# Dilated attention with its first group in natural token order, a selection-product exchange of maxima and sums, and the last head inside the output units

## The reference, cut to what matters

```
for g, (window, dilation) in enumerate(((128, 1), (512, 4), (2048, 16))):
    q = apply_partial_rope(proj[:, :, g, 0], positions) * scale
    k = apply_partial_rope(proj[:, :, g, 1], positions)
    v = proj[:, :, g, 2]
    o, lse = dilated_window_attention(q, k, v, window, dilation)
    outs.append(o); lses.append(lse)
wts = softmax(stack(lses), axis=0)
o = einsum('gbsh,gbshd->bshd', wts, stack(outs))
return o.reshape(B, S, ATTN_WIDTH) @ w_out
```

## Time and profile before

| what | us |
| --- | --- |
| median of 3 runs (2657.55 to 2659.01) | 2658.34 |
| the profiled execution | 2656.87 |
| its span | 2655.1 |
| TensorE busy | 2507.8 (94%) |
| GpSimd busy | 1661.0 (63%) |
| VectorE busy | 1556.2 (59%) |
| ScalarE busy | 481.2 (18%) |

### The profile page before, as it was taken

How to read it: one execution, slowest core, us unless ns; L and a number is a source line. 1 busy time by engine, 2 the same in 40 slices (tenths; PEclk the granted TensorE clock), 3 DMA queues, 4 the chain that set the end, 5 groups by cost and what they waited for, 6 DMA issues and landing times.

```text
span 2655.1 us, 33809 instructions
## 1 busy us (share of the span) xinstructions
PE 2507.8 (94%) x12073; PEld 2028.7 (76%) x12073; DVE 1556.2 (59%) x1655; ACT 481.2 (18%) x832; POOL 1661.0 (63%) x700
## 2 busy tenths in 40 slices
PE   6998999997999997899999989999999998999997
PEld 4776776775888875788888868888887676887886
DVE  5867334685463467767666555434588466644446
ACT  4533221103000003111111121000141442100000
POOL 4435445674777774566666647877777423777784
PEclk7999999997999998999999999999999988999998
DMA  6212343421332322222222213323322101332331
GB/s 242 72 63 70 133 153 115 147 73 56 96 102 87 106 84 85 65 72 79 72 76 74 78 49 95 110 80 95 108 84 88 48 24 48 95 107 83 95 105 54
DMA packets 56332, 236.90 MB, mean 89 GB/s; under 512 B 6528, under 2 KB 7176, under 8 KB 52400
## 3 DMA queue, kind: packets, MB, share of 16 engines
q1 hardware_dynamic: 54720, 230.51, 27.2%
q10 hardware_dynamic: 1520, 5.16, 0.5%
HBM read 233.55 MB, written 2.10 MB: 89 GB/s over the span
## 4 chain that ended last, share of the span: by engine, by line
PE 83%; DVE 8%; ACT 2%; issue 2%; DVEq 2%; ACTq 1%; POOL 1%; DMA 1%; POOLq 0%
PE gg L514 19%; PE gg L515 19%; PE gg L516 19%; PE babcd L551 2%; PE babcd L553 2%; PE babcd L552 2%; PE gg L887 2%; PE be L1022 2%; PE gg L888 1%; PE gg L889 1%; PE babcd L514 1%; PE babcd L515 1%; PE babcd L516 1%; PE babcd L1006 1%; PE babcd L1091 1%
## 5 line engine op out<-in xcount | busy, mean ns | idle before, releaser
L444 POOL TENSOR_TENSOR w_hi<-raw,zero 128x1024 fp32r<-128x1024 f32 (+2 forms) x280 | 585.6, 2092 | 618.3 <-PE gg L516 460.6
L446 POOL TENSOR_TENSOR w_lo<-raw,w_hi 128x1024 fp32r<-128x1024 f32 (+2 forms) x280 | 756.8, 2703 | 39.9
L514 PE MATMUL gg<-h_hi,w_hi 128*128 128x512 f32 x1576 | 627.0, 398 | 9.7 <-ACT ff_s L1437 5.2
L515 PE MATMUL gg<-h_lo,w_hi 128*128 128x512 f32 x1576 | 620.7, 394 | 0.0
L516 PE MATMUL gg<-h_hi,w_lo 128*128 128x512 f32 x1576 | 619.6, 393 | 0.0
L514 PEld LDWEIGHTS gg<-h_hi,w_hi 128*128 128x128 f32 x1576 | 300.3, 191 | 78.5 <-issue 13.1
L516 PEld LDWEIGHTS gg<-h_hi,w_lo 128*128 128x128 f32 x1576 | 300.2, 190 | 63.8
L515 PEld LDWEIGHTS gg<-h_lo,w_hi 128*128 128x128 f32 x1576 | 300.4, 191 | 60.7
L1951 DVE TENSOR_TENSOR ta<-ff_s,gg 128x512 f32<-128x512 f32 x64 | 44.1, 689 | 331.2 <-PE gg L516 323.7
L435 POOL TENSOR_TENSOR w_hi<-raw,zero 128x1536 fp32r<-128x1536 f32 (+2 forms) x48 | 107.2, 2233 | 188.3 <-PE babcd L516 142.3
L514 PE MATMUL gg<-u_hi,w_hi 128*128 128x512 f32 x528 | 209.7, 397 | 4.2 <-issue 4.2
(11 more groups left out here) (530 smaller groups left out, 3998.8 us busy)
## 6 DMA issues: line engine op xcount, KB each, us to landing
raw<-in_w_ff_in_a SPq DMA_DIRECT2D x66, 512.0 KB, 3.6
raw<-in_w_ff_in_b SPq DMA_DIRECT2D x66, 512.0 KB, 3.6
raw<-in_w_att_qk SPq DMA_DIRECT2D x48, 512.0 KB, 3.6
raw<-in_w_ff_out_a SPq DMA_DIRECT2D x24, 704.0 KB, 4.1
raw<-in_w_ff_out_b SPq DMA_DIRECT2D x24, 704.0 KB, 4.1
late_raw<-in_w_ada SPq DMA_DIRECT2D x16, 1024.0 KB, 5.0
raw<-in_w_ml SPq DMA_DIRECT2D x25, 512.0 KB, 3.6
raw<-in_w_merge_a SPq DMA_DIRECT2D x16, 768.0 KB, 5.4
```

The source lines that it names most:

```text
L444: pool.tensor_tensor(hi, a, zero[:].to_broadcast([P, size * P]), ALU.add)
L446: pool.tensor_tensor(lo, a, hi, ALU.subtract).then_inc(S["units_split"], 1)
L514: pe.matmul(dst, w_hi[slot][:, blk], xs[0][:, k, :], start=k == 0, stop=False)
L515: pe.matmul(dst, w_hi[slot][:, blk], xs[1][:, k, :], start=False, stop=False)
```

## The change

The query and key of group 0 are kept in natural token order: projection_out writes them through by_token and by_residue (strided), with rope tables copied into that order. In natural order a block of 128 queries needs two blocks of keys (the first one), so group 0 has 7 blocks a head and groups 1 and 2 have 8: 15 in place of 24. The maxima and sums of the four natural blocks and of the four residues are held by different partitions for the same token. att_swap exchanges them by products with 0/1 matrices (sel_in, sel_out) after swap_in spreads them, and swap_out picks them. ScalarE takes the exp of both shifts (shifts), VectorE merges them (factors), then norm scales the eight parts. The values of group 0 are brought into natural order by four DMAs a head (v_n, from copy_values), and the output of its blocks is written into the residue order by a strided PSUM view. The attention of head h - 1 has its scores after projection unit 0, the exchange after unit 1, the transposes after unit 3 and the values after unit 4 of head h (all one unit later for head 1). The last head's attention runs within the first two output units (last_head). VectorE builds the selection matrices in feed_forward(0), in rope_phase at k == 4 and k == 6. The function tile_mm can be called without its wait.

The diff, cut (removed lines of the old functions are left out; they stand above):

```diff
+        def nat_scores(b):
+            return (ba, bb)[b // 2][:, b % 2 * 256 + (P if b == 0 else 0):b % 2 * 256 + 256]
+        def nat_part(b):
+            return slice(P if b == 0 else 0, 2 * P)
+        def res_scores(r):
+            return (bc, bd)[r // 2][:, r % 2 * 256:r % 2 * 256 + 256]
...
-                wait(pe, "att_scored", h * 4)
...
+            def att_scores(a, p):
+                pe.wait_ge(S["att_roped"], a * 6 + 6)
+                pe.wait_ge(S["att_v_out"], a + 1)
+                for b in range(TB):
+                    mm = pe.matmul(nat_scores(b), qk[p][:, 0, b * P:(b + 1) * P], qk[p][:, 1, max(b - 1, 0) * P:(b + 1) * P],
+                                   start=True, stop=True)
+                mm.then_inc(S["att_scores"], 1)
+                for r in range(4):
+                    tok = slice(r * P, (r + 1) * P)
+                    for n in range(2):
+                        mm = pe.matmul(res_scores(r)[:, n * P:(n + 1) * P], qk[p][:, 2 * n + 2, tok], qk[p][:, 2 * n + 3, tok],
+                                       start=True, stop=True)
+                mm.then_inc(S["att_scores"], 1)
+            def att_swap(a):
+                pe.wait_ge(S["att_expand"], a + 1)
+                y = swap_y[:, 0, :].rearrange("p (x r) -> p x r", x=8)
+                for b in range(TB):
+                    rows = slice(32 * b, 32 * b + 32)
+                    pe.matmul(bf[rows, 0:8], sel_in[:, rows], y[:, b:8:4, :], start=True, stop=True)
+                pe.matmul(bf[:, 8:40], sel_out[:], swap_y[:, 1, :], start=True, stop=True).then_inc(S["att_swapped"], 1)
+            def att_turn(a):
+                for bank, first, last, rows in ((ba, 0, 4, 3), (bb, 4, 7, 4)):
+                    pe.wait_ge(S["att_norm"], a * 8 + rows)
+                    for n in range(first, last):
+                        b, half = (n + 1) // 2, (n + 1) % 2
+                        mm = pe.transpose(bank[:, (n - first) * P:(n - first + 1) * P], p_nat[:, b, half * P:(half + 1) * P], ident[:])
+                    mm.then_inc(S["att_turned"], 1)
+                for q, bank in enumerate((bc, bd)):
+                    pe.wait_ge(S["att_norm"], a * 8 + (2 * q + 6))
+                    for n in range(4):
+                        r, half = 2 * q + n // 2, n % 2
+                        mm = pe.transpose(bank[:, n * P:(n + 1) * P], p_res[:, r, half * P:(half + 1) * P], ident[:])
+                    mm.then_inc(S["att_turned"], 1)
+            def att_values(a, p):
+                wait(pe, "att_o", a)
+                pe.wait_ge(S["att_pt"], a * 4 + 4)
+                pe.wait_ge(S["v_turned"], a * 64 + 64)
+                for r in range(4):
+                    for n in range(2):
+                        pe.matmul(be[:, r * P:(r + 1) * P], v_a[p][:, r, (n + 1) * P:(n + 2) * P], pt_res[:, (2 * r + n) * P:(2 * r + n + 1) * P],
+                                  start=r == 0 and n == 0, stop=False, skip_group_check=True)
+                for n in range(7):
+                    b, half = (n + 1) // 2, (n + 1) % 2
+                    mm = pe.matmul(by_residue(be[:])[:, 32 * b:32 * b + 32, :], v_n[p][:, b - 1 + half, :], pt_nat[:, n * P:(n + 1) * P],
+                                   start=False, stop=n == 6, skip_group_check=True)
                 mm.then_inc(S["att_values"], 1)
...
+            def att_step(a, p, s, at_step):
+                if s == at_step:
+                    att_scores(a, p)
+                if s == at_step + 1:
+                    att_swap(a)
+                if s == at_step + 3:
+                    att_turn(a)
+                if s == at_step + 4:
+                    att_values(a, p)
             def att_two(i):
                 for p in range(2):
                     h = i * 2 + p
                     for s in range(6):
                         if isinstance(h, int) and h == 0:
                             first_head(s)
...
+                            continue
+                        project(h, s)
+                        att_step(h - 1, 1 - p, s, int(isinstance(h, int)))
                     project_values(h)
             peeled(pe, 4, att_two)
...
-            residual("w_att_out", 8, (o_hi, o_lo), RES["att"], between=lambda k: pe.wait_ge(S["att_o"], k + 1))
+            def last_head():
+                u0 = FIRST["w_att_out"]
+                def unit(s, first, last):
+                    ready(u0 + s)
+                    for k in range(first, last):
+                        pe.wait_ge(S["att_o"], k + 1)
+                        tile_mm(g[(u0 + s) % 2], (u0 + s) % 2, k, (o_hi, o_lo))
+                pe.wait_ge(S["att_copied"], 48)
+                att_scores(7, 1)
+                unit(0, 0, 7)
+                att_swap(7)
+                unit(1, 0, 7)
+                att_turn(7)
+                att_values(7, 1)
+                unit(0, 7, 8)
+                unit(1, 7, 8)
+            residual("w_att_out", 8, (o_hi, o_lo), RES["att"], lead=last_head)
...
-            act.dma_start(att_mask[:], t["att_mask"]).then_inc(S["att_consts"], 16)
+            act.dma_start(mask_nat[:, 0:P], t["tri"]).then_inc(S["att_consts"], 16)
+            act.dma_start(mask_nat[:, P:2 * P], t["att_mask"][:, 0, 512:640]).then_inc(S["att_consts"], 16)
+            act.dma_start(mask_res[:], t["att_mask"][:, 0, 512:768]).then_inc(S["att_consts"], 16)
...
-                wait(act, "att_values", h * 4 - 4)
+                wait(act, "att_values", h - 1)
                 for b in range(TB):
                     act.activation(v_a[p][:, b, :], nat[b][:, 0:384], ACT.Copy, scale=colv[:, b:b + 1])
                 act.drain().then_inc(S["att_v_out"], 1)
...
+                wait(act, "att_v_out", h + 1)
+                for b in range(TB):
+                    act.dma_start(v_n[p][:, b, :], v_a[p][32 * b:32 * b + 32, :, 0:P]).then_inc(S["v_turned"], 16)
+            def expo(a):
+                for n in range(8):
+                    part = p_nat[:, n, nat_part(n)] if n < 4 else p_res[:, n - 4, :]
+                    m = n + n // 4 * 4
+                    wait(act, "att_scored", a * 8 + (n + 1))
+                    act.activation(part, part, ACT.Exp, scale=-1.0, bias=a_st[:, m:m + 1],
+                                   accum_out=a_st[:, m + 4:m + 5]).then_inc(S["att_exp"], 1)
+            def shifts(a):
+                wait(act, "att_shift", a + 1)
+                act.activation(a_st[:, 40:56], a_st[:, 40:56], ACT.Exp).then_inc(S["att_fexp"], 1)
+            def turned(a):
+                wait(act, "att_values", a)
+                for n, bank in enumerate((ba, bb[:, 0:3 * P], bc, bd)):
+                    to = (pt_nat[:, 0:4 * P], pt_nat[:, 4 * P:7 * P], pt_res[:, 0:4 * P], pt_res[:, 4 * P:8 * P])[n]
+                    wait(act, "att_turned", a * 4 + (n + 1))
+                    act.activation(to, bank, ACT.Copy).then_inc(S["att_pt"], 1)
+            def att_head(a):
+                expo(a)
+                shifts(a)
+                turned(a)
             def att_two(i):
                 for p in range(2):
                     h = i * 2 + p
...
+                    if not (isinstance(h, int) and h == 0):
+                        att_head(h - 1)
                     copy_values(h, p)
             peeled(act, 4, att_two)
...
+            att_head(7)
...
+            wait(v, "att_consts", 64)
+            v.tensor_copy(by_token(nat_c), by_residue(rope_c[:]))
+            v.tensor_copy(by_token(nat_s), by_residue(rope_s[:]))
+            v.drain()
...
-                v.tensor_tensor(qk[p][:, s, :], bank, rstd[:], ALU.mult)
+                if s < 2:
+                    v.tensor_tensor(by_token(qk[p][:, s, :]), by_residue(bank), by_residue(rstd[:]), ALU.mult)
+                else:
+                    v.tensor_tensor(qk[p][:, s, :], bank, rstd[:], ALU.mult)
                 v.drain().then_inc(S["att_copied"], 1)
             def rotate(h, p, s):
                 q = qk[p][0:32, s, :]
+                cosine, sine = (nat_c, nat_s) if s < 2 else (rope_c[:], rope_s[:])
                 v.stream_shuffle(ra[0], q, SWAP16)
-                v.tensor_tensor(ra[1], q, rope_c[:], ALU.mult)
...
-                v.tensor_tensor(ra[0], ra[0], rope_s[:], ALU.mult)
+                v.tensor_tensor(ra[1], q, cosine, ALU.mult)
+                v.drain()
+                v.tensor_tensor(ra[0], ra[0], sine, ALU.mult)
                 v.drain()
                 v.tensor_tensor(q, ra[0], ra[1], ALU.add)
                 v.drain().then_inc(S["att_roped"], 1)
...
+            def score(a):
+                wait(v, "att_turned", a * 4)
+                for n in range(8):
+                    if n % 4 == 0:
+                        wait(v, "att_scores", a * 2 + (n // 4 + 1))
+                    out, bank, mask = ((p_nat[:, n, nat_part(n)], nat_scores(n), mask_nat[:, nat_part(n)]) if n < 4
+                                       else (p_res[:, n - 4, :], res_scores(n - 4), mask_res[:]))
+                    m = n + n // 4 * 4
```

(123 more changed lines are left out.)

67 lines of the change are left out of this document (31 added, 36 removed).

## The result

The changed kernel takes 2691.8 us (median of 4 runs, 2690.8 to 2696.5) beside 2658.7 us for the kernel before (4 runs, 2657.6 to 2660.0). The ratio is 1.0128, 95% interval 1.011 to 1.0145: 33.1 us more, where 44 were forecast. The spans of the two profiled executions differ by 2690.7 - 2655.1 = 35.6 us.

A forecast was written before the change was run, and what follows sets the result against it. TensorE, busy 94% of the span, was taken as the bound, with VectorE's chain held by GpSimd's splits making it wait. Steady heads +35.4, first +11, last -7.9, strided writes +6.7 gave +45 us: 2702 us, range 2625 to 2724.

The forecast's parts named there:

- The wait at att_turn: Steady heads: TensorE waits for VectorE's norm before the transposes, from 20.7 to 28.8 us after projection 0, 8.1 us.
- The clock: Steady heads: TensorE comes back slow after the wait, 1.4 us lost; the rest of norm delays the transposes 0.4 us.
- What a head saves: TensorE: 9 fewer blocks of scores, transposes and values save 4.8 us, less 0.8 for selection products: net 4.0 us.
- selection products: att_swap's five added TensorE products a head: bounds 0.4 and 1.15 us, 0.8 taken.
- Steady heads: Heads 2 to 7: each +5.9 us from saving, wait and clock, +35.4 us over six stretches.
- Strided writes: Seven value blocks a head writing PSUM with a step of 128 elements: 0.84 us a head, 6.7 us for eight.
- First head: Head 1: later rotations and scores +2.6, att_turn wait some 11, clock 1.4, saved 4.0; sum +11 us.
- Last head: Attention laid within the first two output units: 28.0 us from first scores where it took 35.9, so -7.9 us.
- wait for unit 2's split: After the last head: GpSimd can't split output unit 2 before unit 0's last tile; TensorE waits about 4 us.
- Costed at nothing: v_n transfers, selection tables in feed-forward tiles, mask loads and dropped waits: taken to add no time.
- Sum: Whole kernel: +35.4 + 11 - 7.9 + 6.7 = +45 us, giving 2702 us.
- second rival: att_turn: small instructions slip between GpSimd's, wait only 2 to 5 us, clock stays up; 2642 to 2680 us; chance 0.14.

The follow-up runs named there:

- Few_columns: Changed kernel with GpSimd splitting only 8 columns of each w_att unit, order and waits kept: 2608.9 us.
- all_norm: Changed kernel with rotations and small exchange and factors instructions reading one operand from PSUM, and norm moved from VectorE to ScalarE: 2614.1 us, ratio 0.9835.
- all_psum: Changed kernel with rotations and small exchange and factors instructions reading one operand from PSUM, norm still on VectorE: 2656.1 us.
- before_rot: Kernel before the change, with the rotations of heads 1 to 7 reading one operand of each product from PSUM: 2650.5 us.
- norm_on_act: Changed kernel with norm alone moved from VectorE to ScalarE, rotations and small instructions keeping their SBUF operands: 2688.8 us.

## Why the prediction was right, by its own steps

**The wait at att_turn** is shown. It was forecast from the walk through one head: 8.1 us, from 20.7 to 28.8; measured 7.37, ending at 27.84. The order of events was as written, swap_out held until 14.7 after projection 0, rotate(1) and factors behind. The third product of rotate(1) got in before a split, which I had it wait for, and factors was held longer instead. Few_columns shows that without GpSimd's splits there is no wait, and all_norm that none is left with the splits in place once VectorE's instructions are not held.

**The clock** was undersized. I took 1.4 + 0.4 us a head; what is left of 9.53 beside the wait is 2.2, 1.65 of it the 15 transposes, which took 3.11 us (1327.84 to 1330.95, granted clock 0.50) for 15 x 0.097.

**What a head saves**: 4.0 forecast, 4.29 measured (62.70 - 58.41). The selection products took 0.43 us (0.8 taken, lower bound 0.4).

**Steady heads** therefore cost +31 us over six stretches (1164.64 to 1569.55, for 1155.91 to 1530.06) where I had +35.4: 5.1 us a head for 5.9. One came out at 67.9 us, just below the 68 to 70 named.

**Strided writes** are the term that failed: +6.7 us forecast, nothing measured, in trace and run. VectorE's ratio of 1.54 was the nearest row and does not carry over to TensorE, while VectorE itself pays it in the changed kernel too (projection_out(0), strided, 1.05 us at 1300.30; projection_out(2), packed, 0.69 at 1326.16). The Trainium skill (PSUM — Partial Sum Buffer, Specifications) has any non-contiguous pattern slow a matmul significantly; the 275 ns of both forms contradict that for float32 writes with a step of 128 elements.

**First head**: +11 forecast, 7.3 measured. Its scores began 6.38 us later, of which 1.4 were there before the attention: 5.0 for the 8.1 of the forecast, so -0.6 for +2.6 with the 5.5 us of projection already done. Behind the scores it cost 7.9 (2.4, and the same 5.5) for 8.4. Its att_turn wait was 9.2 for 11.

**Last head**: -7.9 forecast, -3.9 measured from its scores to the sum over rows behind the last output unit (77.1 us for 81.0). The wait for unit 2's split was there (4.2 for 3.8), but unit 2 began 29.3 us after the scores where I had 26.8. Most of these 2.5 us come early: the exchange began at 10.0 us for 8.2, with the granted clock at 0.83 in that stretch (1569.55 to 1579.55) behind a wait of 2.3 us ahead of the scores. Behind unit 2's wait I gave the clock 1.2 us where it takes 3.1.

**Costed at nothing**: that held. The selection tables, the v_n transfers and the masks show up in no wait.

**Sum**: mine +45 = 35.4 + 11 - 7.9 + 6.7. Measured 30.8 + 7.3 - 3.9 + 0 = 34.2, and 1.4 from before the attention make the 35.6 of the two spans. Three terms were too high by 4.6, 3.7 and 6.7 us, and the last head's was wrong by 4.0 the other way, so a part of the closeness is luck. Without the strided term the forecast would have been 2695 us.

**What I missed** is the depth of the bound. My second rival had the wait shrink if instructions slip between splits. The experiments show that moving them trades one wait for another of nearly the same size (6.2 to 6.8 us a head for 7.4), since projection_out(2), the transposes and the next scores all stand on the same VectorE queue. The Trainium skill (SBUF — State Buffer, SBUF: two separate sides) describes the port pair that VectorE and GpSimd share as a lock held for a whole instruction, taken by VectorE instructions that have two SBUF inputs or run in a two-port performance mode. By that, an operand in PSUM sets the two-input ones free, and the runs agree: the 128x8 instruction of factors takes 0.17 us beside a split in all_psum for 1.59 in the changed kernel. No run here tells in which mode norm's tensor_scalar ran, which has one tensor input and is held all the same.

## What to carry to other kernels

When a step is replaced by one that needs more small instructions, price each by what runs beside it, not by its size, and walk the queue in order: here 0.17 us became 2.4. Before moving a held chain, list every consumer that hangs on the same queue; if their times lie within a microsecond or two of each other, reordering gains nothing, and the holding itself has to go, here by an operand in PSUM and by moving norm to ScalarE. A kernel with slack hides such costs (before_rot gained only at the first head), so a change can be charged for something that was there all along.

## What the runs showed of the hardware that was not expected

- Strided float32 matmul writes to PSUM (step 128 elements) cost the same as packed ones, 275 ns; the run with packed writes took the same 2691.8 us.
- VectorE's tensor_scalar on 128x256, four in a row, takes 1.14 us alone (changed kernel) and 4.87 beside a split (all_psum). ScalarE's four scalings of p_nat take 1.61 us beside a split (all_norm, at 1279.5 us) and 1.60 without one (norm_on_act, at 1325.4 us).
- A single 4.2 us wait of TensorE was followed by a granted clock of 0.78 over the next 14 us in the changed kernel. What decides how much a wait costs stays open. In all_psum every head from the second on has the same two waits at the transposes, 1.5 and 2.0 us. One head ran through them at full clock and took 62.26 us, another took 64.77 (the third column from the right is the clock):

```profile
1216.48:1278.74 62.26, 58.84 (x321) 51.99 (x320) 34.08 (x81) 8.29 (x25) 38.28 (x16) 1.00 0.27 81
1407.32:1472.09 64.77, 61.35 (x321) 53.92 (x319) 33.96 (x81) 8.28 (x25) 38.28 (x16) 0.95 0.25 77
```
